# A DeepNorm decoder layer on one core: the stick-breaking stage rebuilt around pairs of heads

## What is computed

```python
def stick_breaking_attention(q, k, v):
    """q, k, v: (B, S, H, d). A[t,s] = beta[t,s] * prod_{s<j<t} (1 - beta[t,j]), s < t."""
    ...
        mask = key_pos[None, :] < q_pos[:, None]
        z = jnp.einsum('bhqd,bhkd->bhqk', q_blk, kf)
        log_beta = jax.nn.log_sigmoid(z)
        log_rem = jnp.where(mask, jax.nn.log_sigmoid(-z), 0.0)
        later = lax.cumsum(log_rem, axis=3, reverse=True) - log_rem
        w = jnp.where(mask, jnp.exp(log_beta + later), 0.0)
        return jnp.einsum('bhqk,bhkd->bhqd', w, vf)
...
        gates = jax.nn.sigmoid(h[..., OFF_GATE:] + b_gate[l]).reshape(B, S, N_BRANCHES, D_MODEL)
        y_sb = stick_breaking_attention(sb_q, sb_k, sb_v).astype(x.dtype) @ w_sb_o[l]
...
        mix = (gates[:, :, 0] * y_sb + gates[:, :, 1] * y_ret) @ w_mix_o[l]
        x = layer_norm(DN_ALPHA * x + mix, ln1_g[l], ln1_b[l])
```

## Time and profile before

| | us |
|---|---|
| median of 3 runs (2229.44 to 2234.68) | 2234.24 |
| the profiled execution, first to last instruction | 2242.3 |
| in it: first stick-breaking projection to first mix matmul | 484.1 (556.04 to 1040.13) |
| PE busy in the whole | 2116.2 (94%) |
| DVE / ACT / POOL busy | 849.7 / 522.8 / 906.4 |

### The profile page before, as it was taken

The page is one execution under the profiler, slowest core; times in us unless marked ns, Lnnn a source line. Parts: engine busy times, 40 slices in busy tenths (PEclk is TensorE's granted clock), DMA queues, the critical chain, the costliest instruction groups (busy, mean ns, idle before and its releaser), DMA issues.

```text
span 2242.3 us, 26283 instructions
## 1 busy us (share of the span) xinstructions
PE 2116.2 (94%) x10280; PEld 1740.1 (78%) x10280; DVE 849.7 (38%) x867; ACT 522.8 (23%) x723; POOL 906.4 (40%) x433
## 2 busy tenths in 40 slices
PE   7999999999999889998978998979999999999995
PEld 6888888788777777787868886858888888888884
DVE  4647457201456282634282224262222121112115
ACT  2312324010335252511143223151100000000013
POOL 4233232344211203044866452974444433444375
PEclk9999999999999998899979999989999999999997
DMA  4111020111100001011112110101111111111112
GB/s 181 42 62 67 26 84 28 47 47 48 38 20 19 29 10 38 1 47 38 52 61 67 65 56 29 47 22 54 47 47 48 55 47 43 51 47 47 49 45 75
DMA packets 31045, 107.96 MB, mean 48 GB/s; under 512 B 3472, under 2 KB 4880, under 8 KB 29968
## 3 DMA queue, kind: packets, MB, share of 16 engines
q1 hardware_dynamic: 27504, 93.50, 12.5%
q10 hardware_dynamic: 3488, 13.70, 1.6%
HBM read 102.99 MB, written 4.19 MB: 48 GB/s over the span
## 4 chain that ended last, share of the span: by engine, by line
PE 85%; DVE 9%; issue 2%; ACT 2%; POOL 1%; DMA 0%; POOLq 0%; ACTq 0%; DVEq 0%
PE unit L398 24%; PE unit L404 24%; PE unit L402 24%; PE unit L376 2%; DVE stick L1270 2%; PE unit L378 1%; PE unit L377 1%; PE aux L524 1%; PE aux L378 1%; PE aux L377 1%; PE aux L376 1%; DVE ln_t L1389 1%; DVE a_lo L1301 1%; DVE beta L1273 1%; ACT stick L904 1%
## 5 line engine op out<-in xcount | busy, mean ns | idle before, releaser
L264 POOL TENSOR_TENSOR w_hi<-w_raw,one 128x1024 fp32r<-128x1024 f32 (+1 forms) x146 | 275.4, 1886 | 1212.4 <-PE unit L398 1177.5
L398 PE MATMUL unit<-x_lo,w_hi 128*128 128x512 f32 x1568 | 613.8, 391 | 17.2 <-POOL w_lo L278 11.1
L402 PE MATMUL unit<-x_hi,w_hi 128*128 128x512 f32 x1568 | 611.4, 390 | 0.0
L404 PE MATMUL unit<-x_hi,w_lo 128*128 128x512 f32 x1568 | 611.4, 390 | 0.0
L267 POOL TENSOR_TENSOR w_lo<-w_raw,w_hi 128x1024 fp32r<-128x1024 f32 (+1 forms) x146 | 360.5, 2469 | 11.4
L398 PEld LDWEIGHTS unit<-x_lo,w_hi 128*128 128x128 f32 x1568 | 295.0, 188 | 81.3 <-POOL w_lo L278 11.1
L404 PEld LDWEIGHTS unit<-x_hi,w_lo 128*128 128x128 f32 x1568 | 295.1, 188 | 62.3
L402 PEld LDWEIGHTS unit<-x_hi,w_hi 128*128 128x128 f32 x1568 | 295.2, 188 | 60.8
L398 PE MATMUL unit<-a_lo,w_hi 128*128 128x512 f32 x608 | 239.5, 394 | 9.8 <-DVE a_lo L1301 9.8
L404 PE MATMUL unit<-a_hi,w_lo 128*128 128x512 f32 x608 | 239.5, 394 | 0.0
L402 PE MATMUL unit<-a_hi,w_hi 128*128 128x512 f32 x608 | 237.5, 391 | 0.0
(11 more groups left out here) (249 smaller groups left out, 3127.5 us busy)
## 6 DMA issues: line engine op xcount, KB each, us to landing
w_raw<-stream SPq DMA_DIRECT2D x156, 512.0 KB, 3.3
rope_sb<-rope ACTq DMA_DIRECT2D x8, 1024.0 KB, 6.0
w_raw<-stream SPq DMA_DIRECT2D x16, 448.0 KB, 3.2
acc<-xT ACTq DMA_DIRECT2D x8, 512.0 KB, 9.7
...
```

Of the source, the lines that this page charges most:

```text
L264: pool.tensor_tensor(w_hi[s][:, 0:width], w_raw[:, s, 0:width], one[:].to_broadcast([P, width]), ALU.mult).then_inc(w_hi_done, 1)
L398: x = pe.matmul(out, w_hi[s][:, wk], lo[:, k, cols], start=first, stop=False, skip_group_check=True)
L402: pe.matmul(out, w_hi[s][:, wk], hi[:, k, cols], start=False, stop=False, skip_group_check=True)
L404: last = pe.matmul(out, w_lo[s][:, wk], hi[:, k, cols], start=False, stop=(k == kts - 1), skip_group_check=True)
```

## The change

- **Step.** A step `g` is a query tile of both heads (32 steps, all written out; no hardware loop is left in this stage). PE's iteration is: `turn_w` of head 0 of step g-1, `logits(g)` of both heads in a run (one `unit` slot each), a fill, `turn_w` of head 1 and `values` of head 0 of step g-1, a fill, `values` of head 1.
- **Fills.** Only the first pair's q, k, v are projected ahead. In steps 0 to 6 of pairs 0 to 2 the next pair's v, k and q are projected between the steps, 12 matmuls of 512 columns in a fill, into `aux` bank 3, in halves of 512 tokens that ACT copies out to the SBUF tile `gate_sb`; two of the 14 fills are 4 transposes of v instead. The last pair's steps 0 to 5 are filled with three gate chunks. Steps 7 of a pair, and steps 6 and 7 of the last, have no fill.
- **Between pairs.** In step 7, ACT and DVE make `sq_hi`, `sk_hi`, `sq_lo`, `sk_lo` of the next pair from SBUF; `logits` of the next pair waits for them.
- **Mask.** The matmul L516 goes (64 in all). DVE adds the triangle in place in PSUM before ACT reads (`mask_z`, 128 columns, once per head and step).
- **The product** `beta * stick` moves from DVE to POOL, which also splits one chunk (two instructions) behind head 0's product in three steps of each pair. `stick` is held once per head.
- **Gate stage.** Five gate chunks instead of four, all ahead of the eight output products.
- Unused semaphores go, the chunks are reordered in the stream, and the -1e30 triangle is loaded at the start.

```diff
+CH_RET, CH_GRET, CH_SB, CH_GSB, CH_MIX, CH_MEM, CH_MO, CH_FFN = 0, 24, 40, 55, 64, 72, 96, 104
+U_RET, U_GRET, U_SB, U_GSB, U_MIX, U_MEM, U_MO, U_FFN = 0, 40, 56, 60, 74, 82, 106, 114
+RU, XU = 10, 6
+STEPS = SB_PAIRS * QT
+EARLY = 3
...
-            split(2, CH_MIX, 8 * P)
+            split(2, CH_SB - 2, 8 * P)
+            for c in range(CH_SB, CH_SB + 4):
+                single(c)
+            pool.wait_ge(stick_edge, 1)
+            for g in range(STEPS):
+                n = (g % QT + 1) * P
+                for hd in range(2):
+                    pool.wait_ge(stick_scanned, 2 * g + hd + 1)
+                    pool.tensor_tensor(beta[:, hd, 0:n], beta[:, hd, 0:n], stick[:, hd, SEQ - n + 1:SEQ + 1], ALU.mult
+                                       ).then_inc(w_ready, 1)
+                    if hd == 0 and g in FILL_STARTS:
+                        single(FILL_STARTS[g] + 1)
+            split(CH_GSB + 1, CH_MIX + 2 - CH_GSB - 1, 8 * P)
...
+            for k in range(3):
+                u = free_unit(U_SB, 0, 0, k)
+                project(CH_SB + k, k % 2, halves(u), x_hi, x_lo).then_inc(unit_ready, 1)
+            pe.wait_ge(unit_drained[0], U_SB // 2 + 2)
+            u = free_unit(U_SB, 0, 0, 3)
+            for b in range(QT):
+                t = pe.transpose(u[:, b * P:(b + 1) * P], next_vT[:, b * P:(b + 1) * P], ident[:])
+            t.then_inc(unit_ready, 1)
+
+            def logits(g):
+                p, qt = divmod(g, QT)
+                q, n = slice(qt * P, (qt + 1) * P), (qt + 1) * P
+                if g == 0:
+                    for j in range(2):
+                        pe.wait_ge(unit_drained[j], U_SB // 2 + 2)
+                pe.wait_ge(z_read, 2 * g)
+                if qt == 0:
+                    pe.wait_ge(qk_split, 2 * p)
+                for hd in range(2):
+                    rows = slice(hd * SB_DIM, (hd + 1) * SB_DIM)
+                    for c0 in range(0, n, HALF):
+                        c1 = min(n, c0 + HALF)
+                        x = triple(unit[:, hd, c0:c1], sq_hi[rows, q], sq_lo[rows, q], sk_hi[rows, c0:c1],
+                                   sk_lo[rows, c0:c1], True, True)
+                    x.then_inc(z_ready, 1)
...
+            def fill(use, piece):
+                kind, c, hf = fill_use(use)
+                if piece == 0:
+                    pe.wait_ge(fill_drained, use)
+                if kind == "turn":
+                    for b in range(4):
+                        x = pe.transpose(aux[:, 3, b * P:(b + 1) * P], next_vT[:, (4 * hf + b) * P:(4 * hf + b + 1) * P],
+                                         ident[:])
+                    x.then_inc(fill_ready, 1)
...
+            for g in range(STEPS + 1):
+                if g:
+                    turn_w(g - 1, 0)
+                if g < STEPS:
+                    logits(g)
+                    for use, piece in fill_slot(g, 0):
+                        fill(use, piece)
+                if g:
+                    turn_w(g - 1, 1)
+                    sb_values(g - 1, 0)
+                if g < STEPS:
+                    for use, piece in fill_slot(g, 1):
+                        fill(use, piece)
+                if g:
+                    sb_values(g - 1, 1)
+
+            pe.wait_ge(z_read, 2 * STEPS)
+            for k in range(4):
+                u = free_unit(U_GSB, 0, 0, k)
+                project(CH_GSB + k, (CH_GSB + k) % 2, halves(u), x_hi, x_lo).then_inc(unit_ready, 1)
+            for hf in range(2):
+                u = free_unit(U_GSB, 0, 0, 4 + hf)
+                project(CH_GSB + 4, CH_GSB % 2, [(u[:, half(hf)], half(hf))], x_hi, x_lo, begins=hf == 0
+                        ).then_inc(unit_ready, 1)
+            for n in range(KT):
+                u = free_unit(U_GSB, 0, 0, 6 + n)
+                c = CH_GSB + 5 + n // 2
+                project(c, c % 2, halves(u), sbo_hi, sbo_lo, kts=4, w0=4 * (n % 2), arrived=sbo_split
+                        ).then_inc(unit_ready, 1)
 
             def spread_rstd(m, hf, counts_chunk=False):
 
...
+            for g in range(STEPS + 1):
+                p, qt = divmod(g, QT)
+                if g:
+                    split_w(g - 1, 0)
+                if g < STEPS:
+                    read_z(g, 0)
+                    for use in fill_ends(g, 0):
+                        drain_fill(use)
+                    if qt == QT - 1 and p < SB_PAIRS - 1:
+                        act.wait_ge(z_ready, 2 * g + 2)
+                        act.wait_ge(fill_drained, 8 * (p + 1))
+                        act.activation(sq_hi[:], next_q, ACT.Copy, scale=SB_DIM ** -0.5).then_inc(qk_hi, 1)
+                        act.activation(sk_hi[:], next_k, ACT.Copy).then_inc(qk_hi, 1)
+                if g:
+                    split_w(g - 1, 1)
+                if g < STEPS:
+                    read_z(g, 1)
+                    for use in fill_ends(g, 1):
+                        drain_fill(use)
+                if g and g % 2 == 0:
+                    pair, two = (g - 1) // QT, (g - 1) % QT // 2
+                    act.wait_ge(sbo_ready, g // 2)
...
+            def mask_z(g, hd):
+                n = (g % QT + 1) * P
+                dve.wait_ge(z_ready, 2 * g + hd + 1)
+                dve.tensor_tensor(unit[:, hd, n - P:n], unit[:, hd, n - P:n], neg[:], ALU.add).then_inc(z_masked, 1)
+
...
+            for g in range(STEPS + 1):
+                p, qt = divmod(g, QT)
+                if g:
+                    split_w(g - 1, 0)
+                if g < STEPS:
+                    mask_z(g, 0)
+                    mask_z(g, 1)
+                    scan(g, 0)
+                    if qt == QT - 1 and p < SB_PAIRS - 1:
+                        dve.wait_ge(qk_hi, 2 * p + 3)
+                        dve.scalar_tensor_tensor(out=sq_lo[:], in0=next_q, scalar=SB_DIM ** -0.5, in1=f32(sq_hi[:]),
+                                                 op0=ALU.mult, op1=ALU.subtract).then_inc(qk_split, 1)
+                        dve.wait_ge(qk_hi, 2 * p + 4)
+                        dve.tensor_tensor(sk_lo[:], next_k, f32(sk_hi[:]), ALU.subtract).then_inc(qk_split, 1)
+                if g:
+                    split_w(g - 1, 1)
+                if g < STEPS:
+                    scan(g, 1)
+                if g and qt == 0 and g < STEPS:
+                    dve.wait_ge(sv_hi_done, p + 1)
+                    dve.tensor_tensor(sv_lo[:].rearrange("p b d -> p (b d)"), next_v,
+                                      f32(sv_hi[:].rearrange("p b d -> p (b d)")), ALU.subtract).then_inc(sv_split, 1)
...
+def fill_use(use):
+
+    p, i = divmod(use, 8)
+    if p == SB_PAIRS - 1:
+        return "gate", CH_SB + 12 + i // 2, i % 2
+    kind, c, hf = (("v", 0, 0), ("v", 0, 1), ("k", 1, 0), ("turn", 0, 0), ("k", 1, 1), ("turn", 0, 1), ("q", 2, 0),
+                   ("q", 2, 1))[i]
+    return kind, CH_SB + 3 + 3 * p + c, hf
+
+
+def fill_slot(g, slot):
+
+    p, qt = divmod(g, QT)
+    if p == SB_PAIRS - 1:
+        return [(8 * p + qt, slot)] if qt < 2 * EARLY else []
+    at = {(0, 0): (0, 0), (0, 1): (0, 1), (1, 0): (1, 0), (1, 1): (1, 1), (2, 0): (2, 0), (2, 1): (2, 1),
+          (3, 0): (3, 0), (3, 1): (4, 0), (4, 0): (4, 1), (4, 1): (5, 0), (5, 0): (6, 0), (5, 1): (6, 1),
+          (6, 0): (7, 0), (6, 1): (7, 1)}
...
+FILL_STARTS = {8 * p + qt: CH_SB + 3 + 3 * p + j for p in range(SB_PAIRS - 1) for j, qt in enumerate((0, 2, 5))}
+FILL_STARTS.update({8 * (SB_PAIRS - 1) + 2 * j: CH_SB + 12 + j for j in range(EARLY)})
+FILLS = 8 * (SB_PAIRS - 1) + 2 * EARLY
...
+    eight += [win[BLK_SB_Q], win[BLK_SB_K], win[BLK_SB_V]]
+    for p in range(1, SB_PAIRS):
+        eight += [win[BLK_SB_V + p], win[BLK_SB_K + p], win[BLK_SB_Q + p]]
+    eight += [win[BLK_GATE_SB + n] for n in range(KT)]
+    eight += [np.concatenate([sb_o[n], sb_o[n + 1]], 1) for n in range(0, KT, 2)]
```

More of the change, by code:

```diff
@@ L92, in layer_program @@
         causal = sb(ctx, "causal", [P, P])
+        neg = sb(ctx, "neg", [P, P])
         ln_ones = sb(ctx, "ln_ones", [P, P], F32R)
@@ new lines, in drain_fill @@
+            def drain_fill(use):
+                kind, c, hf = fill_use(use)
+                act.wait_ge(fill_ready, use + 1)
+                if kind == "gate":
+                    n = c - CH_SB - 12
+                    act.activation(gate_sb[:, n, half(hf)], aux[:, 3, :], ACT.Sigmoid, bias=par[:, 48 + n:49 + n]
+                                   ).then_inc(fill_drained, 1)
+                    return
+                to = {"v": next_vT, "k": next_k, "turn": next_v, "q": next_q}[kind]
+                act.activation(to[:, half(hf)], aux[:, 3, :], ACT.Copy).then_inc(fill_drained, 1)
```

362 lines of the change are left out of this document (133 added, 229 removed).

## The result

| | before | changed |
|---|---|---|
| median (range) of 3 runs, us | 2234.24 (2229.44 to 2234.68) | 2213.73 (2212.59 to 2215.73) |
| ratio, 95% interval | | 0.992 (0.9897 to 0.9942) |
| span of the profiled execution, us | 2242.3 | 2213.8 |
| first stick-breaking projection to first mix matmul, us | 484.1 | 455.65 |

The change makes the kernel 20.5 us faster, 0.8% with an interval clear of 1; 2214 was forecast. One run of the kernel before, 4241 us among those timed beside x4 to x7, was in a slow state and is left out of every figure. The windows of the changed kernel answer to the earlier trace rows: the head, the four pairs, and the gate stage, from 555.85 (first projection) to 1011.50 (first mix matmul).

A forecast was written before the change was run, and what follows sets the result against it. DVE-ACT path was taken to bound wide head-steps, PE narrow ones. Head 37.5 + loop 318.5 + gate stage 99.7 = 455.7 against 484.1 (-28.4); clock +8.5, counted as -20; 2234.2 - 20 = 2214 us, range 2198 to 2234.

The forecast's parts named there:

- Head 37.5: Start of the stage to first logits: three projection chunks, then v copied, turned and split, 37.5 us.
- Branch: PE's loop turning back: its 2.59 us wait goes; slow straight code would show as "issue" rows.
- PE's work in a pair, 71.4: PE in pairs 0 to 2: steps' matmuls 33.1, fills and v's transposes 33.5, gaps 4.8 us.
- The gaps before: Old loop's first pair: 10.9 of 61.6 us put to 16 mask matmuls and shape changes, 0.68 a head-step.
- Wait at a pair's end, 5.3: Step 7, without fill: PE stands 5.3 us before head 1's values; with 0.4 at the next step, 17.1 for three.
- Waits inside a pair, 2 us: Steps 3 and 4, whose fill is only four transposes: 2 us a pair, 6 in all.
- Product on POOL, 2.40 at 1024 columns: The product moved to POOL takes 2.40 us at 1024 columns, priced by POOL's addition of two SBUF tiles.
- rival A: POOL's product is dearer, 3.27 us for 1024 columns: about 10 us in all, 2224; chance 0.15.
- Tail, 10.7 of waits: Last pair's steps without fill: waits of 2.8 us in step 6 and 7.9 in step 7 and drain.
- Clock, +8.5: Five longer stretches with PE mostly idle (head, three pair ends, tail) lose 1.7 us each to the clock.
- Rival C: The change works, but timed runs never had the 12.8 us clock loss: gain only 7 us, 2227; chance 0.12.
- Rivals B and D: B: half clock stays after pair ends, 2244, chance 0.08; D: POOL's start-up binds every step, 2232, chance 0.05.

The follow-up runs named there:

- x4: Changed kernel with the mask back on PE, one 128-column matmul behind each head's logits, and DVE's mask gone: 2239.17 us.
- x7: Changed kernel with heads' logits in turn, head 1's splits first at pair ends, and the last pair's gate fills over all eight steps: 2191.89 us.
- x6: Kernel before with PE's hardware loop over the stage's two double pairs written out: 2236.88 us against 2234.7.
- x5: Changed kernel with 28 unused 512-column matmuls before head 1's values in the last step of pairs 1 to 3: 2205.94 us.
- x1: Changed kernel with the two heads' logits issued in turn, one matmul each, instead of head by head: 2208.17 us.
- x10: Changed kernel with the two heads' logits in turn and both masks on PE behind them: 2210.19 us.
- x2: Changed kernel with head 1's weight splits ahead of the next pair's q and k splits in step 7 of pairs 1 to 3: 2205.12 us.
- x3: Changed kernel with the product beta x scan back on DVE behind each scan, POOL only splitting chunks: 2219.62 us.
- x0: Changed kernel timed again unedited, beside more runs of the kernel before: 2213.2 us, ratio 0.9893 to the kernel before.

## Why the prediction came out right, step by step

- **Head 37.5**: measured 593.33 - 555.85 = 37.5. **Gate stage 99.7**: 100.0. **Branch**: gone, and x6 shows that the loop caused it; the "issue" that the prediction named as a sign of being wrong is the head's wait for `sv_lo`.
- **PE's work in a pair, 71.4: 3.3 too much.** At full clock (x5, second pair) 76.75 us hold 2.1 us of waits and the 6.6 of the added matmuls, so 68.1 remain. Half of the miss is the price of the logits: 12.2 us as columns times pitch, and gaps on top. They take 10.6 us with their gaps, because the two heads overlap in part (x1), which neither the sum nor the rivals had. The other half is the gaps of everything else, 3.1 us instead of 4.8.
- **The gaps before: wrongly named.** Of the 10.9 us that I put down to mask matmuls and changes of shape, 0.68 a head-step, 6.6 stand at the logits and masks (18.8 against 12.2). That is where the gain came from: 8.2 us a pair less for logits and masks, more than the whole 28.4, while the waits grew. x4 says the same from the other side: with the mask back between the heads the rebuilt stage gains nothing, 2239.2 against 2234.7. "The mask goes to DVE" was a clause in my text, and it matters most because it lets the heads stand next to each other; x10 has the mask on PE and keeps the gain. What the removal would give in the kernel before was not run.
- **Wait at a pair's end, 5.3: measured 7.24.** The term that failed is `sk_lo` at 1.23: it took 3.02 beside POOL's product. I had priced it by `sv_lo` of the earlier trace rows, which takes one operand from PSUM; `sk_lo` takes both from SBUF. The earlier trace rows had shown just this for a scan, and I applied it to scans and products but not to the splits behind them. x2 showed how much of it an order could win back.
- **Waits inside a pair, 2 us**: 1.3 (0.47 + 0.52 + 0.28). **Product on POOL, 2.40 at 1024 columns**: 2.00 alone, 2.33 in the mean; rival A's 3.27 did not appear. The move is worth 6.4 us (x3).
- **Tail, 10.7 of waits**: 2.86 + 3.16 + 2.47 = 8.5, and 13.7 us of half clock, for which I had charged 1.7.
- **Clock, +8.5: too low.** x5 took back 7.3 in the median and 8.1 in the trace: 1.4 to 1.7 at each of three pair ends (I said 1.7), 3.5 in the tail. The head's was not tried. Half of PE's busy time in all half-clock stretches of the loop (27.6 us) is 13.8, an upper bound, since part of it lay ahead of waits for other engines.
- **The errors that cancelled.** The sum for the profiled execution was 2242.3 - 20 = 2222; its span was 2213.8, and the stage 28.45 us shorter, which is the forecast without any charge for the clock. The loop with its clock charge was to take 327.0 and took 318.1, 8.9 too much. PE's work and the clock together were to take 284.7 + 8.5 = 293.2 and took 284.1, 9.1 too much: the work was priced too high by more than that, and the clock too low. The waits were to take 33.8 and took 34.0, which is luck: 4.6 too little at the pairs' ends stand against 2.2 too much inside the pairs and 2.2 in the tail. Against the 8.9 stand the 8.1 us that I carried over from "median less span". That difference belonged to the clock of one execution of the kernel before (x0), and the changed kernel has nothing like it: its profiled run took 2215.73, its median is 2213.73. So it is luck that 2214 was met to the microsecond; that the kernel became faster, the head and the gate stage were not luck. Rival C had the mechanism half right: the kernel before loses a varying amount to the clock, and the changed one an almost constant one.
- **Rivals B and D**: no stretch of tens of microseconds at half clock stands in the changed kernel's loop (the longest 13.7), and POOL's start-up is small: its 128-column product took 0.41 us.
